# Spreading the expert weights: which one-hot carries the weight, and in which layout

## The reference, cut to what matters

```python
idx = key1 * 128 + key2                      # from two top-16 lists, 8 heads x 16 picks a token
g = jax.nn.softmax(best_s, axis=-1)
h = einsum('td,ted->te', x, u[idx])
a = gelu(h) * g
out = einsum('te,ted->td', a, v[idx])
```

## Time and profile before

| what | value |
|---|---|
| median of 3 runs | 3316.73 us (3316.06 to 3318.95) |
| profiled execution | 3322.88 us |
| its span | 3321.2 us |
| mean granted TensorE clock | 0.943 |
| e_tab matmuls | 1536, first start 1161.3, last 1709.2 us |
| e_left instructions | 192; shortest, median, longest 671, 678, 695 ns |
| e_right instructions with w_hi | 768; 296, 302, 2232 ns |

### The profile page before, as it was taken

The page is one execution under the profiler, slowest core; times in us unless marked ns, Lnnn a source line. Parts: engine busy times, 40 slices in busy tenths (PEclk is TensorE's granted clock), DMA queues, the critical chain, the costliest instruction groups (busy, mean ns, idle before and its releaser), DMA issues. The chain is left out here.

```text
span 3321.2 us, 50919 instructions
## 1 busy us (share of the span) xinstructions
PE 3068.7 (92%) x17450; PEld 1716.5 (52%) x17450; DVE 2621.2 (79%) x5543; ACT 1005.1 (30%) x1471; POOL 1286.2 (39%) x891
## 2 busy tenths in 40 slices
PE   8898899889888499999986999999999999999999
PEld 4444555445444266666653555555555554444444
DVE  3235455429999999999967888888888888999996
ACT  4322255333332255554522222222222222222221
POOL 1021111012432322111226666666655555556652
PEclk9998557999999799999997999999999999999999
DMA  3210100121110144444448887888888888888885
GB/s 106 64 38 1 51 1 1 45 83 59 54 51 34 51 160 166 172 178 161 182 183 293 294 275 275 279 290 274 275 281 283 272 273 278 305 297 305 296 297 181
DMA packets 256173, 594.90 MB, mean 179 GB/s; under 512 B 20768, under 2 KB 127408, under 8 KB 252976
## 3 DMA queue, kind: packets, MB, share of 16 engines
q1 hardware_dynamic: 180016, 318.63, 28.4%
q0 software_dynamic: 73728, 268.47, 22.8%
q10 hardware_dynamic: 2304, 6.29, 0.5%
HBM read 513.63 MB, written 79.69 MB: 179 GB/s over the span
## 5 line engine op out<-in xcount | busy, mean ns | idle before, releaser
L238 PE MATMUL f_y<-f_v_hi,f_a_hi 128*128 128x512 f16 x1536 | 583.3, 380 | 11.8 <-DVE p_h L2172 11.7
L239 PE MATMUL f_y<-f_v_lo,f_a_hi 128*128 128x512 f16 x1536 | 583.2, 380 | 0.0
L240 PE MATMUL f_y<-f_v_hi,f_a_lo 128*128 128x512 f16 x1536 | 583.2, 380 | 0.0
L2139 POOL DMA_INDIRECT f_rows<-in_peer_u,p_row_index x256 | 353.3, 1380 | 211.8 <-DVE f_rows L2180 129.4
L2139 POOL DMA_INDIRECT f_rows<-in_peer_v,p_row_index x256 | 311.0, 1215 | 281.8 <-DVE p_h L2190 253.6
L2180 DVE SCALAR_TENSOR_TENSOR f_rows<-f_rows,p_xs 128x1024 f32<-128x1024 f32 x256 | 380.0, 1517 | 49.3 <-DMA f_rows<-in_peer_u,p_row_index 49.2
L2190 DVE SCALAR_TENSOR_TENSOR p_h<-f_rows,f_row_a,p_h 128x1024 f32<-128x1024 f32 x256 | 394.7, 1542 | 18.7 <-DMA f_rows<-in_peer_v,p_row_index 11.9
L2172 DVE SCALAR_TENSOR_TENSOR p_h<-f_y,p_h 128x512 f32<-128x512 f32 x384 | 263.0, 685 | 106.6 <-PE f_y L240 104.4
L2150 POOL TENSOR_TENSOR f_v_lo<-f_v_in,f_v_hi 128x1024 f16<-128x1024 f32 x128 | 282.1, 2204 | 144.1 <-ACT f_v_hi L2114 143.0
L238 PE MATMUL f_hid<-p_act_hi,x_u_hi 128*128 128x384 f16 x1008 | 330.2, 328 | 2.0 <-DVEq L2157 2.0
L239 PE MATMUL f_hid<-p_act_lo,x_u_hi 128*128 128x384 f16 x1008 | 330.2, 328 | 0.0
(11 more groups left out here) (299 smaller groups left out, 5606.3 us busy)
## 6 DMA issues: line engine op xcount, KB each, us to landing
f_v_in<-in_peer_v SPq DMA_DIRECT2D x128, 512.0 KB, 5.2
dense_weights<-e_stage SPq DMA_DIRECT2D x24, 2048.0 KB, 8.7
f_g_in<-dense_weights SPq DMA_DIRECT2D x32, 1536.0 KB, 15.7
x_u_in<-in_peer_u SPq DMA_DIRECT2D x64, 512.0 KB, 4.8
e_u_in<-in_peer_u SPq DMA_DIRECT2D x48, 512.0 KB, 4.2
x_gel<-early_tiles SPq DMA_DIRECT2D x64, 384.0 KB, 3.5
early_tiles<-e_gel SPq DMA_DIRECT2D x48, 384.0 KB, 2.5
a_w_in<-in_w_in SPq DMA_DIRECT2D x24, 512.0 KB, 3.9
```

The costliest lines, as they stand in the source:

```text
L238: pe.matmul(out, a_hi, b_hi, start=first, stop=False)
L239: pe.matmul(out, a_hi, b_lo, start=False, stop=False)
L240: return pe.matmul(out, a_lo, b_hi, start=False, stop=last)
L2139: nc.gpsimd.indirect_dma_start(out=rows[q % ROWS][:], out_offset=None, in_=table, in_offset=bass.IndirectOffsetOnAxis(ap=T.row_index[:, ti ...
```

## The change

The roles of the two one-hots are exchanged. The weight now rides on the one-hots of key2, which stay the stationary side, and the plain one-hots of key1 are the moving side. The weighted one-hots are laid out with the token innermost, [key2 value, 4 tokens], so that 16-bit copies of key2 and of the two weight parts can be used as second tensors in instructions that cover all four tokens. A step on DVE is now four instructions of 512 elements each:

- same: e_iota (f16, each number repeated for 4 tokens) compared with key2 (f16), into one of two tiles;
- right: T.iota compared with key1 (both f32), after the wait on spread;
- left high and left low: same times w_hi and same times w_lo, all f16, after a wait on same's own completion (semaphore same_done).

The matmul's stationary operand is left[r][:, part, :, j], whose 128 elements lie 4 elements apart. Ahead of the loop key2 is cast to f16, and w_lo is a tile of its own in f16.

```diff
@@ -1745,14 +1745,17 @@
     with ExitStack() as ctx:
         S = Space(nc, ctx, "e")
         E = EarlyTiles(nc, io, T, S, EARLY_S, EARLY_R * PEER_H, EARLY_S * NBLOCK)
-        iota = S.sb("iota", [P, P], F16)
-        left = [S.sb(f"left{r}", [P, BANK_T, P], F16) for r in range(RING)]
-        right = [S.sb(f"right{r}", [P, 2, BANK_T, P], F16) for r in range(RING)]
-        w_hi16 = S.sb("w_hi16", [P, DSEQ], F16)
-        w_hi = S.sb("w_hi", [P, DSEQ])
+
+
+        iota = S.sb("iota", [P, P, BANK_T], F16)
+        same = [S.sb(f"same{r}", [P, P, BANK_T], F16) for r in range(2)]
+        left = [S.sb(f"left{r}", [P, 2, P, BANK_T], F16) for r in range(RING)]
+        right = [S.sb(f"right{r}", [P, BANK_T, P], F16) for r in range(RING)]
+        key2, w_hi, w_lo = (S.sb(n, [P, DSEQ], F16) for n in ("key2", "w_hi", "w_lo"))
         stage = [S.sb(f"stage{b}", [P, NKEYS, TB]) for b in range(2)]
         tab = [S.ps(f"tab{r}", [P, BANK_T, P]) for r in range(RING)]
         vec_step = S.sem("vec_step")
+        same_done = S.sem("same_done")
         built = S.sem("built")
         spread = S.sem("spread")
         out = S.sem("out")
@@ -1764,33 +1767,33 @@
         next_lo = S.sem("next_lo")
         next_hidden = S.sem("next_hidden")
         block = ctx.enter_context(nc.Block())
-        key1_t, key2_t, w_lo = T.picked_t
+        key1_t, key2_t, w_t = T.picked_t
 
         HALVES = {(r * STEPS + 1) // (2 * EARLY_S): (r // 2, r % 2) for r in range(2 * EARLY_S)}
 
         @block.vector
         def _(dve):
             c = Chain(dve, vec_step)
-            c.link(nc.vector.tensor_scalar(w_lo, w_lo, S_G, None, ALU.mult))
-            c.step(nc.vector.tensor_copy(iota[:], T.iota[:]))
-            c.link(nc.vector.tensor_copy(w_hi16[:], w_lo))
-            c.link(nc.vector.tensor_copy(w_hi[:], w_hi16[:]))
-            c.link(nc.vector.tensor_tensor(w_lo, w_lo, w_hi[:], ALU.subtract))
+            c.step(nc.vector.tensor_scalar(w_t, w_t, S_G, None, ALU.mult))
+            c.step(nc.vector.tensor_copy(iota[:], lanes(T.iota[:], 2, P, P, BANK_T)))
+            c.link(nc.vector.tensor_copy(key2[:], key2_t))
+            c.link(nc.vector.tensor_copy(w_hi[:], w_t))
+            c.link(nc.vector.tensor_tensor(w_lo[:], w_t, w_hi[:], ALU.subtract))
             with dve.Fori(0, NBLOCK) as blk:
                 for s in range(STEPS):
                     r = s % RING
-
+                    toks = bass.ds(blk * BLOCK + s * BANK_T, BANK_T)
+
+                    def each(x):
+                        return lanes(x[:, toks], 1, P, P, BANK_T)
+
+                    nc.vector.tensor_tensor(same[s % 2][:], iota[:], each(key2), ALU.is_equal).then_inc(same_done, 1)
                     dve.wait_ge(spread, BASE - RING + 1 + blk * STEPS + s)
-                    nc.vector.tensor_tensor(left[r][:], lanes(T.iota[:], 1, P, BANK_T, P),
-                                            lanes(key2_t[:, bass.ds(blk * BLOCK + s * BANK_T, BANK_T)], 2, P, BANK_T, P),
-                                            ALU.is_equal)
-                    for j in range(BANK_T):
-                        tok = bass.ds(blk * BLOCK + (s * BANK_T + j), 1)
-                        nc.vector.tensor_scalar(right[r][:, 0, j, :], iota[:], key1_t[:, tok], w_hi[:, tok],
-                                                ALU.is_equal, ALU.mult)
-                        last = nc.vector.tensor_scalar(right[r][:, 1, j, :], iota[:], key1_t[:, tok], w_lo[:, tok],
-                                                       ALU.is_equal, ALU.mult)
-                    last.then_inc(built, 1)
+                    nc.vector.tensor_tensor(right[r][:], lanes(T.iota[:], 1, P, BANK_T, P),
+                                            lanes(key1_t[:, toks], 2, P, BANK_T, P), ALU.is_equal)
+                    dve.wait_ge(same_done, blk * STEPS + s + 1)
+                    nc.vector.tensor_tensor(left[r][:, 0], same[s % 2][:], each(w_hi), ALU.mult)
+                    nc.vector.tensor_tensor(left[r][:, 1], same[s % 2][:], each(w_lo), ALU.mult).then_inc(built, 1)
             for b in range(2):
                 dve.wait_ge(next_hi, b + 1)
                 nc.vector.scalar_tensor_tensor(F.u_lo[b][:], E.u_ps[:], S_U, F.u_hi[b][:], ALU.mult,
@@ -1808,7 +1811,7 @@
                     pe.wait_ge(out, BASE - RING + 1 + n)
                     for j in range(BANK_T):
                         for part in range(2):
-                            mm = pe.matmul(tab[r][:, j, :], left[r][:, j, :], right[r][:, part, j, :],
+                            mm = pe.matmul(tab[r][:, j, :], left[r][:, part, :, j], right[r][:, j, :],
                                            start=part == 0, stop=part == 1)
                     mm.then_inc(spread, 1)
                     if s in HALVES:
```

## The result

The changed kernel takes 3281.36 us (median of 4 runs, 3279.75 to 3283.85), the kernel before beside it 3317.84 us. The ratio is 0.9891, with a 95% interval of 0.9874 to 0.9908: 1.1% faster, 36.5 us, where 41 had been forecast.

What follows compares the result with a forecast made beforehand. DVE was taken to bound the spread stage, with PE next. The 42.1 us ceiling less about 1 gave 41; 3322.9 - 41 = 3281.9 profiled, 6.2 less unprofiled: 3276 us, range 3268 to 3322.

Steps and rivals of the forecast that it cites:

- DVE sets the pace: Spread stage before the change: DVE is busy for all of a block's 45.64 us, PE for 42.55.
- PE's floor: Spread stage: PE alone needs 41.9 us a block, so a faster DVE gives at most 3.7 us a block.
- The price of an all-16-bit two-input instruction: DVE's same and two weight products, 512 elements each: 0.33 us apiece, with 0.60 as upper bound.
- Rival C: DVE finds no faster pace with two inputs: 0.60 us an instruction, 4 us more, 3321 us; chance 0.12.
- The stalls: DVE's waits for POOL's e_u_lo, four a block, 7.5 us in all, kept unchanged; DVE's block becomes 32.9 us.
- Strided weights: PE's e_tab weight loads, read with a step of 4 elements: 0 to 5 ns more each.
- Sum: 41 us: Spread stage ends 41 us earlier: 42.1 us less about 1 us.
- about 1 us for tab groups that catch a DVE stall or a slower load: PE's e_tab groups in the spread stage: about 1 us taken off the 42.1 us gain.
- the ceiling of 42.1: Most the spread stage can gain, counted from PE's first hidden matmul at 1165.17: end at 1667.1 against 1709.2.
- 3276 us: Forecast median of the unprofiled runs: 3281.9 us for the profiled execution, less 6.2.

Runs made afterwards that it cites:

- experiment 2: Changed kernel with key2, w_hi and w_lo in f32 (3414.35 us), plus one 2-element single-input DVE copy in every step: 3340.41 us, ratio 1.006.
- experiment 3: Changed kernel with DVE waiting once, ahead of its second step, until POOL's first e_u_lo is done: 3275.59 us, ratio 0.9875; run again, 3267.99 us.

## Why the prediction came out as it did

- *DVE sets the pace, PE's floor is 41.9 us a block.* Right: 41.87, reached in two ways.
- *The price of an all-16-bit two-input instruction, 0.33 us.* Right: 0.33. Rival C's price, 0.60, came true with f32 operands, but not its time: at that price POOL's e_u_lo is kept out, and the kernel loses 97 us where I had 4.
- *The stalls stay at 7.5 us a block.* Wrong, and harmless after the start: POOL now runs in DVE's pauses, and DVE is busy for 27.1 us a block where I had 32.9. The sentence behind it, that of the two the later one waits for the earlier one in both directions, is what failed; experiment 2 shows POOL, ready at 1341.14, waiting through three instructions that began after that and the one then running. The Trainium skill has it my way ("SBUF — State Buffer", Who interferes with whom: whoever issues first gets the shared pair for the whole instruction, and the other one blocks); by that the f32 e_u_lo would have waited for one instruction of 0.6 us and not for 12.2 us, so the rows of the spread stage differ from it; those of the experts stage agree.
- *Strided weights cost 0 to 5 ns.* Right: nothing at a step of 4.
- *Sum: 41 us.* The stage gained 37.0. The "about 1 us for tab groups that catch a DVE stall or a slower load" measured nothing: no e_tab matmul waited, and their pitch stayed 56 ns. The term that failed stands in the ceiling of 42.1: it holds PE's start at 1165.17, that is, it puts the effect of the change on the first e_u_lo at nothing. It cost 5.7 us. PE's first hidden matmul came 19.3 us after the r_bank transposes in place of 15.2, which is 4.1; and PE then ran 17 matmuls in place of 7 at the lower clock (a pitch of 0.32 us in place of 0.16), which is 1.6. The rest of the ceiling was 0.6 us too low (experiment 3), and 42.1 + 0.6 - 5.7 is the 37.0. I had named that e_u_lo as what starts PE, and did not ask whether DVE's faster row would hold it up. Experiment 3 takes the loss away and gets 5.5 to 5.7 us back. Why it was 17 matmuls stays open: with key2 in f32 PE waited longer, 6.1 us, and ran 11.
- *3276 us.* The median was 3281.4, and the profiled execution 3279.75 where 3281.9 had been worked out. That last agreement is luck: the stages ahead happened to be 7.6 us faster in this execution.

## What to carry to other kernels

Work out both engines' floors per loop turn before pricing a speed-up: here 12.3 us off DVE were worth 3.8, and the same 3.8 lay in POOL's four visits alone. When single-input DVE instructions are replaced by two-input ones, ask which POOL instruction shares the stage and where it will get in. Here one wait at the start was worth 5.5 us, and one tiny copy a step 74 us in the kernel that had no pauses; the copy was not tried in the changed kernel, where DVE pauses anyway. Compare a stage from two fixed instructions of the trace when other stages scatter by more than the effect.

## What the runs showed of the hardware that was not expected

- In the spread stage DVE instructions with two SBUF inputs, back to back, kept a POOL instruction that reads SBUF out for up to 12.3 us (a record of 14.4 for 2.1 us of work). It got in at a pause of DVE or at a single-input instruction. In the experts stage it got in between two two-input instructions. What decides this was not tried.
- A weight load of 128 x 128 f16 with a step between its elements: records of 98, 113, 146 and 150 ns for steps of 2, 8, 16 and 64 bytes; the pitch of the matmuls above it 56, 56, 62 and 64 ns.
- The stages ahead scatter by 14.5 us between executions with the same code: their last transposes began between 1136.7 and 1151.2 us. The granted clock goes with it. From 400 to 600 us it was 0.78 in the four profiles where they began between 1136.7 and 1139.4, 0.72 to 0.74 in the five with 1142.4 to 1147.3, and 0.70 in the three with 1149.2 to 1151.2, that of the kernel before among them.
